# Two gated feed-forwards with seven block products per weight unit in place of eight, on one core of a Trainium2

## The reference, cut to what matters

```python
def swiglu_ffn(x, w_gate, w_up, w_down):
    return (jax.nn.silu(x @ w_gate) * (x @ w_up)) @ w_down
...
        y = swiglu_ffn(x, ffn_wg[l], ffn_wu[l], ffn_wd[l])
        x = layer_norm(ALPHA * x + y, ln_ffn_g[l], ln_ffn_b[l])
```

## Time and profile before

| | |
|---|---|
| median of 3 runs | 2422.56 us (2421.21 to 2422.78) |
| span of the profiled execution | 2419.9 us, 28651 instructions |
| PE, matmuls | 2386.0 us busy, 99% |
| PE, weight loads | 1944.4 us, 80% |
| DVE | 1448.5 us, 60% |
| ACT | 873.7 us, 36% |
| stage ffn0, first to last matmul | 413.1 to 773.1 us |
| stage ffn1, first to last matmul | 959.6 to 1320.9 us |

### The profile page before, as it was taken

How to read it: one execution, slowest core, us unless ns; L and a number is a source line. 1 busy time by engine, 2 the same in 40 slices (tenths; PEclk the granted TensorE clock), 3 DMA queues, 4 the chain that set the end, 5 groups by cost and what they waited for, 6 DMA issues and landing times.

```text
span 2419.9 us, 28651 instructions
## 1 busy us (share of the span) xinstructions
PE 2386.0 (99%) x11134; PEld 1944.4 (80%) x11134; DVE 1448.5 (60%) x1994; ACT 873.7 (36%) x1230; POOL 22.7 (1%) x39
## 2 busy tenths in 40 slices
PE   8999999999999999999999999999999999999998
PEld 7887888888887887888887786888888777888886
DVE  6997646444446846444446725565566776665566
ACT  4455445222223834322223625422122465222122
POOL 0000000000000000000000000000000000000000
PEclk9999999999999999999999999999999999999999
DMA  5222312322222211222222220233333211222221
GB/s 183 105 101 92 122 35 105 114 104 88 103 88 103 77 64 70 105 97 94 97 94 102 77 105 35 83 109 118 120 112 120 87 53 64 93 96 95 104 90 66
DMA packets 38811, 228.06 MB, mean 94 GB/s; under 512 B 8837, under 2 KB 8917, under 8 KB 12496
## 3 DMA queue, kind: packets, MB, share of 16 engines
q1 hardware_dynamic: 31680, 219.17, 25.3%
q0 software_dynamic: 7056, 7.86, 1.3%
HBM read 221.71 MB, written 5.24 MB: 94 GB/s over the span
## 4 chain that ended last, share of the span: by engine, by line
PE 86%; DVE 7%; ACT 5%; issue 1%; DMA 1%; SPq 0%; DVEq 0%; ACTq 0%
PE bank L710 85%; DVE w_lo L2074 2%; ACT w_hi L1483 1%; DMA w_raw<-weights_in 1%; ACT xs L1564 1%; ACT xh L1502 1%; DVE xl L2089 1%; DVE cacc L2310 1%; PE bank L1414 1%; DVE xs L2204 0%; DVE xs L2184 0%; ACT pr L1806 0%; DVE sum_x L2096 0%; DVE sum_q L2103 0%; DVE xs L2160 0%
## 5 line engine op out<-in xcount | busy, mean ns | idle before, releaser
L2074 DVE TENSOR_TENSOR w_lo<-w_raw,w_hi 128x2048 fp32r<-128x2048 f32 x200 | 458.2, 2291 | 372.7 <-ACT w_hi L1483 372.6
L710 PE MATMUL bank<-xh,w_hi 128*128 128x512 f32 x1408 | 553.6, 393 | 13.3 <-DVE w_lo L2532 6.7
L710 PE MATMUL bank<-xl,w_hi 128*128 128x512 f32 x1408 | 548.9, 390 | 0.0
L710 PE MATMUL bank<-xh,w_lo 128*128 128x512 f32 x1408 | 548.8, 390 | 0.0
L1483 ACT ACTIVATE w_hi<-w_raw 128x2048 fp32r<-128x2048 f32 x200 | 381.6, 1908 | 400.1 <-PE bank L710 394.1
L2160 DVE TENSOR_TENSOR xs<-xs,bank 128x512 f32<-128x512 f32 x448 | 294.5, 684 | 102.1 <-PE bank L710 101.1
L710 PEld LDWEIGHTS bank<-xh,w_hi 128*128 128x128 f32 x1408 | 264.8, 188 | 77.2 <-DVE w_lo L2532 6.7
L710 PEld LDWEIGHTS bank<-xh,w_lo 128*128 128x128 f32 x1408 | 264.8, 188 | 55.4
L710 PEld LDWEIGHTS bank<-xl,w_hi 128*128 128x128 f32 x1408 | 265.0, 188 | 54.3 <-issue 0.5
L710 PE MATMUL bank<-yh,w_hi 128*128 128x512 f32 x576 | 227.2, 394 | 0.4 <-DVE w_lo L2074 0.3
L710 PE MATMUL bank<-yl,w_hi 128*128 128x512 f32 x576 | 224.3, 389 | 0.0
(11 more groups left out here) (299 smaller groups left out, 2868.3 us busy)
## 6 DMA issues: line engine op xcount, KB each, us to landing
w_raw<-weights_in SPq DMA_DIRECT2D x204, 1024.0 KB, 4.8
rel_scratch<-vt POOLq DMA_DIRECT2D x8, 384.0 KB, 19.9
bias<-rel_scratch POOLq DMA_DIRECT2D x8, 256.0 KB, 3.2
y_out<-xs SPq DMA_DIRECT2D x8, 256.0 KB, 2.2
xs<-x_in SPq DMA_DIRECT2D x3, 512.0 KB, 8.7
mk<-mem_in POOLq DMA_DIRECT2D x1, 1024.0 KB, 7.3
window<-consts_in POOLq DMA_DIRECT2D x1, 576.0 KB, 6.4
xs<-x_in SPq DMA_DIRECT2D x2, 256.0 KB, 4.5
```

What stands on the lines that cost most here:

```text
L710: return pe.matmul(dst, a, b, start=start, stop=stop)
L2074: dve.tensor_tensor(w_lo[:, slot(c), :], w_raw[:, c % 2, :], w_hi[:, slot(c), :].bitcast(F32), ALU.subtract)\
```

## The change

The first chunk keeps its plain gate and up units. The 20 gate and up units of chunks 1 to 10 are each treated as a product of 2x2 blocks: the weights' 1024x256 block is cut by even and odd feature tile and by output tile (each block 512 features by 128 columns), the activations by even and odd feature tile and by token half (512 features by 256 tokens). Seven block products replace eight, each of 4 feature tiles by 3 matmuls of 256 columns: 84 matmuls of 256 columns in place of 48 of 512.

The four sums of activation blocks are made once per stage (DVE `feature_sums` and `rest_of_sums`, ACT `give_high_sums`; tiles `st`, `sh`, `sl`). Of each weight unit four blocks enter as sums: DVE's `weight_sums` makes them in three steps (1024, 512 and 512 elements a partition) into `tw`, ACT's `high_t` makes their high parts in `w_hi` (2048), DVE's `rest_of_t` the low parts (2048, and this counts up `w_lo_ready`). Three blocks enter as they are: ACT's `high_parts` makes `eh` (1536) and DVE's `rest_of_parts` makes `el` (1536). The products add up in half banks: ACT's `copy_part` takes an intermediate result out of a bank three times in a unit while PE works on another bank, and a fourth time at the unit's end (256 columns each, `part_full`, `part_copied`), and PE waits for copy 0 before its 4th product, copy 1 before its 6th and copy 2 before its 7th. DVE's `join` puts each half together (two of 512 a unit), ACT's `gate_half` does Silu from SBUF, DVE's `hidden_half` the product.

Down units now span two chunks' 512 hidden rows and half of the 1024 columns (`half_down`, dA and dB): again 48 matmuls of 512 columns, but 4 output tiles in place of 8, so half the adds. The order in the loop (now four trips) is dA, dB, up, gate, up, gate. The stage ends with dA, dB, the up unit of chunk 10, and then the plain down unit of chunk 10. Scaling the residual moves from DVE to ACT (two of 2048), POOL's load of `window` from unit 1 of ffn0 to unit 29 (a change of the unit count that it waits for). The host packs the weights to match; the number and size of the loads stay as they are. Other stages are not touched.

The diff, cut to the order of the work on each engine (`U` is the stage's first unit, `n` counts seven-product units):

```diff
+        c = U + 5
+        loop(SEVEN_TRIPS, 6, half_down("t", "dA", c) + half_down("t", "dB", c + 1) + seven("tb", "u", c + 2)
+             + seven("ta", "g", c + 3) + seven("ta", "u", c + 4) + seven("tb", "g", c + 5))
+        c = U + 5 + 6 * SEVEN_TRIPS
+        straight(half_down("e", "dA", c) + half_down("e", "dB", c + 1) + seven("e", "u", c + 2))
+        straight(downs(name, "last", c + 3))
...
-            pool.wait_ge(unit_used, UNITS["ffn0"] + 1)
+            pool.wait_ge(unit_used, UNITS["ffn0"] + 29)
...
+                def sevenfold(tag, which, c, n, i=None):
...
+                    key = (name, tag, which)
+                    y, z, w_, x_ = seven_banks(key)
...
+                    def copied(j):
+                        pe.wait_ge(sem["part_copied"], at(i, 16, 4 * (first_seven + n) + j))
+
+                    pe.wait_ge(w_lo_ready, at(i, 6, c + 1))
+                    wait_free(pe, key + (1,), i)
+                    product(x_, b_block(1), quarter(0, 0), start=True).then_inc(sem["part_full"], 1)
+                    wait_free(pe, key + (0,), i)
+                    product(z, t_block(1), sums(S1), start=True)
+                    product(y, b_block(2), quarter(1, 0)).then_inc(sem["part_full"], 1)
+                    copied(1)
+                    product(x_, t_block(2), sums(S2))
+                    product(w_, t_block(3), quarter(1, 1)).then_inc(sem["part_full"], 1)
+                    copied(2)
+                    product(z, b_block(0), sums(S4)).then_inc(sem["part_full"], 1)
+                    copied(3)
+                    full(product(x_, t_block(0), sums(S3)), key + (1,))
+
+                def half_down(tag, which, c, chunk, i=None):
+
+                    pe.wait_ge(w_lo_ready, at(i, 6, c + 1))
+                    pe.wait_ge(sem["h_ready"], at(i, 4, 2 * (base + chunk)))
+                    for m in range(4):
+                        key = (name, tag, which, m)
+                        wait_free(pe, key, i)
+                        for k in range(4):
+                            last = mm3(bank(key)[:, :], weights(c, k * T + m * P, P),
+                                       (fhh[:, k // 2, :, k % 2, :], fhl[:, k // 2, :, k % 2, :]), k == 0, k == 3)
+                        full(last, key)
...
+
+                plain(U, "g", ready)
+                plain(U + 1, "u")
+                pe.wait_ge(sem["sums_ready"], 2 * (int(name[3]) + 1))
+                sevenfold("p1", "g", U + 2, 0)
+                sevenfold("p1", "u", U + 3, 1)
+                sevenfold("p2", "g", U + 4, 2)
+                c = U + 5
+                with pe.Fori(0, SEVEN_TRIPS) as i:
+                    half_down("t", "dA", c, 2, i)
+                    half_down("t", "dB", c + 1, 2, i)
+                    sevenfold("tb", "u", c + 2, 3, i)
+                    sevenfold("ta", "g", c + 3, 4, i)
+                    sevenfold("ta", "u", c + 4, 5, i)
+                    sevenfold("tb", "g", c + 5, 6, i)
+                c = U + 5 + 6 * SEVEN_TRIPS
+                half_down("e", "dA", c, 2 + 2 * SEVEN_TRIPS)
+                half_down("e", "dB", c + 1, 2 + 2 * SEVEN_TRIPS)
+                sevenfold("e", "u", c + 2, SEVENS - 1)
+                last_down(c + 3)
...
+                def high_parts(c, n, i=None):
+
+                    act.wait_ge(raw_loaded[c % 2], at(i, 48, 16 * (c // 2 + 1)))
+                    act.wait_ge(unit_used, at(i, 6, c - 1))
+                    act.activation(part_hi[(c - U) % 2][:, :], w_raw[:, c % 2, 0:3 * T], ACT.Copy).then_inc(sem["part_hi"], 1)
+
+                def high_t(c, n, sums, i=None):
+
+                    act.wait_ge(sem["t_ready"], at(i, 4, first_seven + n + 1))
+                    act.activation(quarters(w_hi[:, slot(c), :]), sums, ACT.Copy).then_inc(w_hi_ready, 1)
...
+                def copy_part(tag, which, n, j, c=None, i=None):
...
+                    g = 0 if which == "g" else 1
+                    if j == 3:
+                        act.wait_ge(unit_used, at(i, 6, c + 1))
+                    else:
+                        act.wait_ge(sem["part_full"], at(i, 16, 4 * (first_seven + n) + j + 1))
+                    src = z if j == 1 else x_
+                    to = (sn[:, g, 0, 0, :], sn[:, g, 1, 1, :], sn[:, g, 0, 1, :], sn[:, g, 1, 0, :])[j]
+                    act.activation(to, src, ACT.Copy, scale=-1.0 if j == 2 else 1.0).then_inc(sem["part_copied"], 1)
...
+                def gate_half(tag, half, i=None):
+                    wait_drained(act, (name, tag, "g", half), i)
+                    act.activation(sn[:, 0, half, :, :], sn[:, 0, half, :, :], ACT.Silu).then_inc(sem["sil_ready"], 1)
...
+                def high_half(chunk, half, i=None):
+                    act.wait_ge(sem["h_made"], at(i, 4, 2 * ((FFN_CHUNKS - 1) * l + chunk - 1) + half + 1))
+                    act.activation(fhh[:, chunk % 2, half, :, :], sn[:, 1, half, :, :], ACT.Copy).then_inc(sem["hh_ready"], 1)
...
+                def during_up(tag, c, n, chunk, i=None, nxt=None, gate=None):
+
+                    if nxt is not None:
+                        high_parts(nxt, n + 1, i)
+                    copy_part(tag, "u", n, 0, i=i)
+                    if gate:
+                        gate_half(gate, 1, i)
+                    copy_part(tag, "u", n, 1, i=i)
+                    if nxt is not None:
+                        high_t(nxt, n + 1, t_sums, i)
+                    copy_part(tag, "u", n, 2, i=i)
+                    high_half(chunk, 0, i)
+                    copy_part(tag, "u", n, 3, c, i)
...
+                def before_down(tag, c, n, chunk, i=None):
+
+                    split_hi(c + 1, i, 6)
+                    copy_part(tag, "g", n, 0, i=i)
+                    high_half(chunk, 1, i)
+                    for j in range(1, 3):
+                        copy_part(tag, "g", n, j, i=i)
+                    gate_half(tag, 0, i)
+                    copy_part(tag, "g", n, 3, c, i)
+                    gate_half(tag, 1, i)
...
+                def during_downs(c, n, i=None):
+
+                    split_hi(c + 1, i, 6)
+                    high_parts(c + 2, n, i)
+                    high_t(c + 2, n, t_sums, i)
...
+                with act.Fori(0, SEVEN_TRIPS) as i:
+                    during_downs(c, 3, i)
+                    during_up("tb", c + 2, 3, 2, i, nxt=c + 3)
+                    high_parts(c + 4, 5, i)
+                    copy_part("ta", "g", 4, 0, i=i)
+                    high_half(2, 1, i)
+                    copy_part("ta", "g", 4, 1, i=i)
+                    high_t(c + 4, 5, t_sums, i)
+                    copy_part("ta", "g", 4, 2, i=i)
+                    gate_half("ta", 0, i)
+                    copy_part("ta", "g", 4, 3, c + 3, i)
+                    during_up("ta", c + 4, 5, 3, i, nxt=c + 5, gate="ta")
+                    before_down("tb", c + 5, 6, 3, i)
...
+                def weight_sums(c, n, sums, i=None, after=None):
...
+                    raw = quarters(w_raw[:, c % 2, :])
+                    dve.wait_ge(raw_loaded[c % 2], at(i, 48, 16 * (c // 2 + 1)))
+                    if after is not None:
+                        dve.wait_ge(w_lo_ready, at(i, 6, after + 1))
+                    dve.tensor_tensor(sums[:, 0:4, :].rearrange("p (a q) t -> p a q t", a=2),
+                                      raw[:, 0:4, :].rearrange("p (a q) t -> p a q t", a=2),
+                                      raw[:, 6:8, :].unsqueeze(1).broadcast_to([P, 2, 2, HT]), ALU.add).then_inc(sem["t_step"], 1)
+                    dve.wait_ge(sem["t_step"], at(i, 8, 2 * (first_seven + n) + 1))
+                    dve.tensor_tensor(sums[:, 4:6, :], sums[:, 2:4, :], raw[:, 0:2, :], ALU.add).then_inc(sem["t_step"], 1)
+                    dve.wait_ge(sem["t_step"], at(i, 8, 2 * (first_seven + n) + 2))
+                    dve.scalar_tensor_tensor(sums[:, 6:8, :], sums[:, 4:6, :], -1.0, raw[:, 4:6, :], ALU.mult, ALU.subtract)\
+                       .then_inc(sem["t_ready"], 1)
...
+                def join(tag, which, n, half, i=None):
...
+                    dve.wait_ge(sem["part_copied"], at(i, 16, 4 * (first_seven + n) + 3 + half))
+                    if half == 0:
+                        dve.wait_ge(sem["part_full"], at(i, 16, 4 * (first_seven + n) + 4))
+                    p_ = sn[:, g, half, :, :]
+                    b_ = bank(key)[:, :].rearrange("p (a t) -> p a t", a=2)
+                    free(dve.tensor_tensor(p_, p_, b_, ALU.subtract if half else ALU.add), key)
...
+                def up(tag, n, chunk, i=None):
+                    for half in range(2):
+                        join(tag, "u", n, half, i)
+                        hidden_half(tag, half, chunk, i)
...
+                def downs_and_up(tag, c, n, chunk, i=None, last=False):
+
+                    split_lo(c + 1, i, 6)
...
+                    if last:
+                        split_lo(c + 3)
+                        half_adds(tag, "dB", range(3, 4), i)
+                    else:
```

(36 more changed lines are left out.)

249 lines of the change are left out of this document (239 added, 10 removed).

## The result

| | |
|---|---|
| before, median of 4 runs | 2421.94 us (2421.21 to 2422.78) |
| after, median of 4 runs | 2437.72 us (2437.07 to 2438.56) |
| ratio | 1.0066, 95% interval 1.0052 to 1.0080 |
| span of the profiled execution after | 2435.3 us, granted clock 0.993 over the span (before 2419.9, 0.999) |

The account below looks back on a forecast made before the run. PE at its matmul pace was taken to bound the gated stages. A stage gains 16.2 us and loses 20.1, 3.9 slower; 7.6 was taken for both, moving the median from 2422.6 to 2430.2 us, range 2416 to 2441.

Parts of the forecast that it names:

- gain: PE's 20 seven-product units a stage: 10.07 us each in place of 10.88, so 16.2 us less a stage.
- Wait 1: Stage's start: PE waits for DVE's sums and low parts before the third unit, 5.0 us with the restart.
- Wait 2: First up unit: its copy 0 comes behind the gate unit's joins, so PE waits 0.8 us with the restart.
- Waits 3: Four loop trips: PE waits for copy 0 behind two DVE-ACT chains (11.4 and 10.9 against 10.1); 10.2 us a stage.
- Wait 4: Stage's end: the last down unit waits for the last chunk's hidden tiles, 4.1 us with the restart.
- the clock: PE's granted clock behind the new pauses: the sum charged nothing for a fall, leaving it to rival B.
- Nothing for: No cost for halved down-unit adds, DVE's share, weight loads (over 5 us early) or POOL's later load of window.
- rival B: Much slower: the clock falls behind the four start and end pauses, 8 to 16 us, 2438 to 2446; chance 0.17.
- Rival A: Faster: the loop's two waits do not come about, the chain being under 10.1; 12.6 us gained in both, 2410; chance 0.12.
- Rival C: Slower: register-count waits and operands cut in four cost 0.05 more on a trip's 20 steps; 2440; chance 0.15.
- Rival D: The Trainium skill's formula holds: each product 0.13 us shorter, waits grow by most of it; 2410 to 2420; chance 0.03.
- The likeliest case: The forecast itself: both gated stages slower, median 2430.2 us, own range 2424 to 2435; chance 0.53.

Follow-up runs that it names:

- experiment 7: Changed kernel with the DVE and ACT reordering of experiment 4 and the thrown-away matmuls of experiment 1 in the four pauses; 2409.1 us, ratio 0.9944.
- experiment 1: Changed kernel plus thrown-away matmuls in PE's four pauses, 20 before each stage's third unit and 18 before its last down unit; 2428.0 us, ratio 1.0028.
- experiment 3: Changed kernel with ACT's copy 0 of each up unit and of the loop's gate unit ta ahead of the next high part; 2430.5 us, ratio 1.004.
- experiment 2: Changed kernel plus 8 thrown-away matmuls at each of PE's four pauses; 2431.51 us, ratio 1.004.
- experiment 4: The reordered loop: experiment 3 plus three moves on DVE and one on ACT, with an added wait on ACT; 2415.06 us, ratio 0.9973.
- experiment 5: Changed kernel with ends rearranged: third unit starts with plain-block products, last down unit's first four tiles go by token half; 2428.87 us, ratio 1.0026.
- experiment 6: Changed kernel with the reordered loop of experiment 4 and the rearranged stage ends of experiment 5 together; 2405.78 us, ratio 0.9933.
- experiment 8: Experiment 6 plus ACT's copy 0 of the first seven-product unit ahead of the first chunk's two high parts; 2405.55 us, ratio 0.9928.

## Why the prediction was right, and where it was not

Its sum, step by step for one stage, against ffn0:

| step | forecast | shown |
|---|---|---|
| gain | 16.2 | a trip without waits is 62.10 against 62.04: gain 15.9 |
| Wait 1 | 5.0 | 15.70 between the starts of two units less 10.88: 4.8 |
| Wait 2 | 0.8 | 46.73 - 46.00 = 0.7 |
| Waits 3 | 10.2 | 257.83 - 248.40 = 9.4 |
| Wait 4 | 4.1 | 766.40 - 762.17 less one slot of 0.12: 4.1 |
| the clock | 0 | 356.92 - 352.38 = 4.5 |
| stage | +3.9 | +7.8 |

The steps shown come to 7.6; 0.2 is not placed.

- **The gain** was right to 0.1 us a trip. The 0.1199 of the earlier trace rows carried over; with the count of products (1.36 us a unit), or with the formula that the prediction quotes from the Trainium skill ("TensorE: Matmul & The Clock Gate", "Back-to-back issue gap"; 109 ns, 1.2 us a unit), the same list of waits would have made it a faster kernel.
- **Waits 1, 3 and 4** came at the places named, with the engine named and within 0.8 us. Durations of single rows and hand-offs of 0.03 to 0.04 us, added up along one chain, were good enough to forecast waits that no row of before showed. The one term that was too high is the further 0.1 us for a release by ACT: the copy ends at 510.18 and PE starts at 510.23, no later than behind DVE. Over the eight waits of four trips that is the difference of 10.2 and 9.4.
- **Luck in Waits 3.** The ten durations of the longer chain, with the corrections that the prediction names, come to 11.2 and not to 11.4 (11.4 less 0.4 plus 0.24), which would be a wait of 1.2 (11.2 less 10.1) in place of 1.4; PE was 1.45 late (1.29 idle and 0.16 under the last matmul). What the terms lack lies mostly at the chain's head: copy 1 starts 0.20 us behind the last slot of product 3 (498.90 against 498.70), where the sum has 0.04.
- **Nothing for** the weight loads and for `window` was right: in ffn0 the only wait on a DMA that the profile names is one of 2.2 us on ACT, 1.9 before, and PE never waits for one.
- **The step that failed** is the clock: the sum held it at zero and put the fall aside as rival B, with a chance of 0.17 "mostly with one or two of the four falling". All four fell. The price given was "2 us and up to twice that" each; measured it was 2.0 and 2.3 at the starts and 2.5 and 2.6 at the ends, near its lower bound. The hint was in the earlier trace rows: matmuls 0.43 apart behind 6.72 us without work. It is a weaker hint than the prediction makes of it, since that is the start of the program, and the profile's own clock reads 1.00 there (window 6.72 to 11.16). But the longest other pause in the trace of before is 1.99 us, so no row had a pause of 4 or 5 us with the clock kept either, and holding the clock at zero had no row behind it. By the prediction's own price (8 to 16 for four falls) the sum would have been 2438 to 2446; with the 9 us measured it would have been 2439.
- **Rival A** (no waits in the loop) did not come about, though its price was about right: 10.2 us a stage against the 9.4 that the reordered loop gave, and the kernel of experiment 7, with no wait in the loop and no fall of the clock in the stages, takes 2409.1 us where A had 2410. What keeps it from happening is the order on DVE and ACT, not the length of their work.
- **Rival C** did not come about: ACT's 507.63 follows DVE's product (506.90 and 0.69) by 0.04, with a count from a register between. **Rival D** falls with the trip of 62.10.

The likeliest case and rival B together describe what happened; each alone does not. The time lies in the range because the range reached into B, not because the sum had it: the waits were right, and more than half of the 15.8 us came from a term that stood at nothing.

## What to carry to other kernels

When a change cuts the bottleneck's work and adds serial work beside it, price the gain by the distance between starts at the new size, and lay out the chain that each new wait hangs on. Then look at the order of that chain before giving up the change: here the same instructions in another order turned +0.66% into -0.27%, and with shorter pauses at the stage's ends into -0.67%. A pause of PE of 2 us and more can cost more than its length: look at the granted clock behind it, count 1 to 3 us for a fall (0.9 to 2.6 here), and fill or split the pause if it can't go.

## What the runs showed of the hardware

- In the gated stages the granted clock fell behind PE pauses of 4.5, 3.96, 3.35 and 2.71 us in every case, behind 2.45 us in one of two, and behind 2.11 and 1.84 us and less never. No kernel here kept the clock up over a pause longer than 2.45 us.
- That is no safe limit. At about 230 us, in a stage that no edit touches, PE pauses for 1.99 or 2.00 us in all ten profiled executions. The clock stayed up behind it in four (before, after, experiments 1 and 3) and fell in six (experiments 2 and 4 to 8). Before, and then experiment 6:

```profile
230.41 0.50 PE L710 MATMUL bank<-xh,w_hi 128*128 128x512 f32 x1 [1.99 <-DVE xl L2089]
230.00:235.00 5.00, 4.59 (x20) 3.49 (x21) 3.64 (x6) 4.89 (x7) 0.00 (x0) 1.00 0.01 3
```
```profile
229.68 0.50 PE L766 MATMUL bank<-xh,w_hi 128*128 128x512 f32 x1 [2.00 <-DVE xl L2405]
230.00:235.00 5.00, 5.00 (x16) 3.95 (x15) 2.90 (x5) 4.32 (x6) 0.00 (x0) 0.66 0.02 3
```

- At the lower level the matmuls stood 0.213 (256 columns) and 0.43 us (512) apart, in place of 0.120 and 0.227. The price of a fall is not fixed. Behind the same pause of 4.5 us it was 2.0 us at the changed kernel's start and 1.5 at the reordered one's (47.48 less 46.00); behind the same 3.35 us it was 2.3 at the end of ffn0 and 0.9 at the end of ffn1, both in experiment 4 (49.97 and 48.61 less 47.68). In the changed kernel the second matmul behind the first start's pause was already slow (439.88 to 440.09 us); in the reordered one the second to fifth still stood 0.12 apart:

```profile
441.39 0.28 PE L1205 MATMUL bank<-xh,eh 128*128 128x256 f32 x1
441.51 0.35 PE L1205 MATMUL bank<-xl,eh 128*128 128x256 f32 x1
441.65 0.41 PE L1205 MATMUL bank<-xh,el 128*128 128x256 f32 x1
441.86 0.42 PE L1205 MATMUL bank<-xh,eh 128*128 128x256 f32 x1
```

- The second unit of ffn0, up to which no experiment edits anything, started between 423.8 and 426.4 us in the ten profiled executions. Most of that spread is the fall at 230 us: from the first matmul behind that pause to this unit it is 194.1 to 194.3 us in the four executions that kept the clock and 195.5 to 195.8 in the six that did not. Differences of 1 to 2 us between two spans are therefore no evidence; the three-part table above does not depend on it.
